# Lag blocks by way of memory and POOL's queue instead of PE, and a convolution part moved ahead, in an S5 and PEER step

## The reference

```python
def s5_scan(u, h0, ...):        # diagonal complex state space, one direction
    bu = einsum("gnp,blgp->blgn", b_bar, u)
    a_cum, h = associative_scan(_combine, (a, bu), reverse=reverse, axis=1)
    h = h + a_cum * h0
    return einsum("gpn,blgn->blgp", c_mat, h).real, ...

y = y_f + y_b + d_skip * u                   # 32 groups of 16 channels
g = gelu(y);  out = g * sigmoid(g @ w_glu + b_glu)
y_conv = cb * short_conv(cc * ch, conv_w, conv_b)      # z = h @ w_in gives u, cb, cc, ch
y = concat(rmsnorm(out), rmsnorm_heads(y_conv)) @ w_out ;  x = x + g1 * y
x = x + g2 * peer(rmsnorm_mod(x))            # top-k of keys, 16 of 16384 experts per head
```

## Time and profile before

| | |
|---|---|
| median of 3 runs | 1924.06 us (1923.41 to 1924.34) |
| the profiled execution, its own time | 1922.27 us |
| its span, first to last instruction | 1920.1 us |
| PE busy | 1194.3 us, 62% |
| DVE busy | 1382.6 us, 72% |
| ACT busy | 373.5 us, 19% |
| POOL busy | 725.1 us, 38% |
| mean DMA rate | 392 GB/s |
| first gather of the PEER stage | at 215.58 us |

### The profile page before, as it was taken

One profiled execution on the slowest core, in us unless ns is written; L12 is line 12 of the kernel. 1 busy time (PEld: TensorE's weight loads), 2 busy tenths in 40 slices (PEclk: granted clock), 3 DMA queues, 4 the chain that ended last, 5 costly groups with the idle time before them and its releaser, 6 DMA issues.

```text
span 1920.1 us, 21154 instructions
## 1 busy us (share of the span) xinstructions
PE 1194.3 (62%) x7716; PEld 475.8 (25%) x7716; DVE 1382.6 (72%) x3664; ACT 373.5 (19%) x845; POOL 725.1 (38%) x666
## 2 busy tenths in 40 slices
PE   6989898999777777775543343544343454444434
PEld 3569644444322322221110000111000011111001
DVE  8968567777766766669777776677777678766664
ACT  5142441121122121111211110121111121111110
POOL 0000233344444434445434444444444354444440
PEclk9999999999878877775755555565555565555555
DMA  9855699999999999999999999999999999999994
GB/s 372 328 209 199 257 395 414 378 416 420 390 421 399 419 422 421 420 389 422 420 422 423 421 421 421 421 421 421 422 422 421 421 421 418 422 420 421 418 420 182
DMA packets 120968, 753.16 MB, mean 392 GB/s; under 512 B 12240, under 2 KB 27856, under 8 KB 33568
## 3 DMA queue, kind: packets, MB, share of 16 engines
q0 software_dynamic: 92160, 671.13, 84.5%
q1 hardware_dynamic: 28704, 80.69, 11.0%
HBM read 749.12 MB, written 11.04 MB: 396 GB/s over the span
## 4 chain that ended last, share of the span: by engine, by line
DMA 43%; PE 28%; DVE 23%; issue 2%; POOL 1%; ACT 1%; SPq 0%; DVEq 0%; POOLq 0%; ACTq 0%
DMA r<-table,gidx 31%; DVE r L1747 9%; DMA mix_r<-table,gidx 8%; PE bank L878 7%; PE bank L846 6%; PE bank L983 3%; DMA r<-w_mod 3%; DVE mix_r L1747 2%; PE bank L996 2%; PE bank L813 1%; POOL r L1935 1%; PE bank L962 1%; PE bank L855 1%; DVE i L1680 1%; PE bank L788 1%
## 5 line engine op out<-in xcount | busy, mean ns | idle before, releaser
L1935 POOL DMA_INDIRECT r<-table,gidx x542 | 607.7, 1121 | 865.3 <-PE bank L878 723.9
L1747 DVE CUSTOM_DVE_ANT_0 r<-r 128x1024 f32<-128x1024 f32 x542 | 658.1, 1220 | 246.5 <-DMA r<-table,gidx 246.0
L878 PE MATMUL bank<-r,cond 128*32 128x512 f32 x1432 | 327.2, 911 | 370.4 <-DVE cond L1759 295.2
L878 PE MATMUL bank<-r,wgt 128*32 128x512 f32 x736 | 166.8, 921 | 194.1 <-DVE wgt L1759 145.8
L1289 ACT ACTIVATE r<-r 128x2 f32<-128x2 f32 x320 | 65.1, 204 | 1013.1 <-DVE r L1747 1012.5
L878 PEld LDWEIGHTS bank<-r,cond 128*32 128x32 f32 x1432 | 37.1, 129 | 572.0 <-DVE cond L1759 437.2
L1935 POOL DMA_INDIRECT mix_r<-table,gidx x98 | 109.4, 1116 | 136.1 <-PE bank L878 117.0
L1747 DVE CUSTOM_DVE_ANT_0 mix_r<-mix_r,r 128x1024 f32<-128x1024 f32 x98 | 119.3, 1221 | 48.4 <-DMA mix_r<-table,gidx 48.2
L878 PE MATMUL bank<-mix_r,cond 128*32 128x512 f32 x264 | 91.1, 994 | 80.7 <-DVE cond L1759 63.4
L846 PE MATMUL bank<-hT_r,r 128*128 128x512 f32 x256 | 121.5, 630 | 0.9 <-ACT hT_r L1143 0.9
L878 PEld LDWEIGHTS bank<-r,wgt 128*32 128x32 f32 x736 | 18.9, 130 | 295.3 <-DVE wgt L1759 214.3
(11 more groups left out here) (367 smaller groups left out, 1637.1 us busy)
## 6 DMA issues: line engine op xcount, KB each, us to landing
r<-w_mod SPq DMA_DIRECT2D x24, 1024.0 KB, 9.7
r<-wq_heads SPq DMA_DIRECT2D x14, 1024.0 KB, 8.8
r<-table,gidx POOLq DMA_INDIRECT x542, 18.7
wq_heads<-w_query SPq DMA_DIRECT2D x8, 1024.0 KB, 12.1
r<-w_tiles SPq DMA_DIRECT2D x12, 512.0 KB, 7.8
x_r<-w_tiles SPq DMA_DIRECT2D x10, 512.0 KB, 6.0
hT_r<-xT SPq DMA_DIRECT2D x4, 640.0 KB, 6.1
r<-w_u SPq DMA_DIRECT2D x1, 2048.0 KB, 29.5
```

Of the source, the lines that this page charges most:

```text
L878: last = mm(bank[ACC[b % 2][h]][to:to + TG, :], pair_weights(NPR * G + g)[:, e, :], rows[SLOT[G * TOPK + k]][:, D + h * 512:D + (h + 1) * ...
L1747: V.tensor_tensor_reduce(row, row, h2r[tg], 1.0, 0.0, ALU.mult, ALU.add, hid[:, par, k:k + 1]).then_inc(dot_done, 1)
L1935: G_.indirect_dma_start(rows[SLOT[j]], None, table, bass.IndirectOffsetOnAxis(gidx[:, e, k:k + 1], 0)).then_inc(row_in[SLOT[j]], 16)
```

## The change

Four things are done together.

1. PE computes the products of the lag blocks before the chunk sums instead of after them, and DVE's `lag_blocks()` stands ahead of the scan instead of between its third and fourth step.
2. M is no longer made by PE and ACT. POOL writes `Ksb` to `kfull` in device memory with one DMA (512 pieces of 960 bytes), waits for it, and reads it back with 8 DMAs, each into 16 rows of M (16 x 32 pieces of 512 bytes, 0.26 MB). PE waits for all nine ahead of the context's output.
3. The odd steps 9, 11, 13 and 15 of the chunk sums are evicted by DVE (`s_back`) instead of ACT. In each scan step two products over half the width become one over the full width, with the halves read in reverse.
4. `conv_ctx(0)` moves from behind the context's output to ahead of it, ahead of slabs 20 to 22. ACT's copy `ccx` moves with it.

```diff
@@ SP
-            sp.wait_ge(m_mm, 2)
+            sp.wait_ge(lag_dma, 16)
             sp.dma_start(wqa, w_query[:, :, 0:DQ]).then_inc(ld_first, 16)
@@ PE
             mod_slab(16)
 
-            pe.wait_ge(bpt_ev, 17)
-            for g in range(16):
-                if g >= 2:
-                    pe.wait_ge(s_ev, g - 1)
...
             pe.wait_ge(bd_ready, 1)
             pe.wait_ge(cp_ready, 1)
             pe.wait_ge(dm_ready, 1)
...
                 last.then_inc(k_mm, 1)
+
+            pe.wait_ge(bpt_ev, 17)
+            for g in range(16):
+                if g >= 10 and g % 2:
+                    pe.wait_ge(s_back, (g - 9) // 2)
+                elif g >= 2:
+                    pe.wait_ge(s_ev, min(g - 1, 4 + g // 2))
...
+                last.then_inc(s_mm, 1)
+                if g == 7:
+                    mod_slab(17)
             mod_slab(18)
             mod_slab(19)
-            pe.wait_ge(k_ev, 1)
-            pe.wait_ge(s_ev, 16)
-            for a in range(2):
-                for s in range(Q):
...
-                last.then_inc(m_mm, 1)
-                mod_slab(20 + a)
-            mod_slab(22)
...
-                pe.wait_ge(m_ev, (1, 2, 5)[r])
...
-            pe.wait_ge(m_ev, 8)
+            conv_ctx(0)
+            mod_slab(20)
+            mod_slab(21)
+            mod_slab(22)
+            pe.wait_ge(lag_dma, 16 * (Q + 1))
+            pe.wait_ge(s_ev, 12)
+            pe.wait_ge(s_back, 4)
+            pe.wait_ge(k_ev, 1)
             pe.wait_ge(hbc_ready, 1)
...
-            conv_ctx(0)
             pe.wait_ge(yc_gelu, 2)
@@ ACT
-            for g in range(16):
+            for g in (*range(8), *range(8, 16, 2)):
...
-            for n in range(8):
-                a, j = n // 4, n % 4
-                act.wait_ge(m_mm, a + 1)
-                A(M[:, 2 * j + a::8, :], bank[MBANK[a][j]][:, :].rearrange("p (q x) -> p q x", q=4), ACT.Copy).then_inc(m_ev, 1)
+            act.wait_ge(zc_mm, 4)
+            A(ccx.rearrange("p k t -> p (k t)"), bank[0][:, :], ACT.Copy).then_inc(ccx_ev, 1)
             act.wait_ge(scan_ctx, 1)
...
-            act.wait_ge(zc_mm, 4)
-            A(ccx.rearrange("p k t -> p (k t)"), bank[0][:, :], ACT.Copy).then_inc(ccx_ev, 1)
@@ DVE
-                link(tt(ta, prev, re, ALU.mult),
-                     tt(tb[:, :, 0, :], prev[:, :, 1, :], im[:, :, 0, :], ALU.mult),
-                     tt(tb[:, :, 1, :], prev[:, :, 0, :], im[:, :, 1, :], ALU.mult))
+                link(tt(ta, prev, re, ALU.mult), tt(tb, prev[:, :, ::-1, :], im, ALU.mult))
...
-            dve.wait_ge(s_ev, 16)
+            lag_blocks()
+            for g in range(9, 16, 2):
+                pr = g % 8 * 2
+                dve.wait_ge(s_mm, g + 1)
+                for r in range(2):
+                    src = bank[4 + g % 2][:, 0:4 * NCH].rearrange("p (q r c) -> p c r q", q=2, r=2)[:, :, r, :]
+                    V.tensor_copy(HH[:, NCC:0:-1, r, 1, pr:pr + 2], src[:, 0:NCC, :])
+                    last = V.tensor_copy(HH[:, NCH - 1:NCC:-1, r, 1, pr:pr + 2], src[:, NCC + 1:NCH, :])
+                last.then_inc(s_back, 1)
+            dve.wait_ge(s_back, 4)
+            dve.wait_ge(s_ev, 12)
...
-                if i == 3:
-                    lag_blocks()
...
-                     tt(seg_b[:, :, 0, :], last[:, :, 1, :], PI, ALU.mult), tt(seg_b[:, :, 1, :], last[:, :, 0, :], PI, ALU.mult))
+                     tt(seg_b, last[:, :, ::-1, :], PI.rearrange("p i (a x) -> p i a x", a=1).broadcast_to([P, SEG, 2, NQ]), ALU.mult))
@@ POOL
             pool.sem_inc(bd_ready, 1)
 
+            pool.wait_ge(k_ev, 1)
+            G_.dma_start(kfull.rearrange("(m p) x -> p m x", p=P), Ksb).then_inc(lag_dma, 16)
+            pool.wait_ge(s_mm, 8)
+            pool.wait_ge(lag_dma, 16)
+            lags = kfull.rearrange("(g i) x -> i g x", i=GC)
+            for i in range(Q):
+                G_.dma_start(M[GC * i:GC * i + GC, :, :], lags[:, :, (Q - 1 - i) * GC:(Q - 1 - i) * GC + P]).then_inc(lag_dma, 16)
+
             pool.wait_ge(mod_tr, 6)
```

More of the change, by code:

```diff
@@ L291, in build @@
         d_mm = sem("d_mm")
-        m_mm = sem("m_mm")
-        m_ev = sem("m_ev")
+        lag_dma = sem("lag_dma")
+        s_back = sem("s_back")
         s_mm = sem("s_mm")
@@ L621, in _ @@
             mod_slab(16)
-            pe.wait_ge(bpt_ev, 17)
-            for g in range(16):
-                if g >= 2:
-                    pe.wait_ge(s_ev, g - 1)
-                for j in range(2):
-                    q = 2 * g + j
-                    for r in range(2):
-                        for a in range(2):
[L631 to L635, removed]
             pe.wait_ge(bd_ready, 1)
@@ L647, in _ @@
                 last.then_inc(k_mm, 1)
+            pe.wait_ge(bpt_ev, 17)
[4 more added lines that the diff above has]
+                    pe.wait_ge(s_ev, min(g - 1, 4 + g // 2))
+                for j in range(2):
+                    q = 2 * g + j
+                    for r in range(2):
+                        for a in range(2):
+                            last = mm(bank[4 + g % 2][64 * a:64 * a + 64, (2 * j + r) * NCH:(2 * j + r + 1) * NCH],
+                                      BPT[:, q, r, 64 * a:64 * a + 64], U[:, 2 * (q % NPAIR) + a, :], start=True, stop=True)
+                last.then_inc(s_mm, 1)
+                if g == 7:
+                    mod_slab(17)
             mod_slab(18)
             mod_slab(19)
-            pe.wait_ge(k_ev, 1)
-            pe.wait_ge(s_ev, 16)
-            for a in range(2):
-                for s in range(Q):
[L656 to L663, removed]
-                last.then_inc(m_mm, 1)
-                mod_slab(20 + a)
-            mod_slab(22)
             def conv_ctx(r):
-                pe.wait_ge(m_ev, (1, 2, 5)[r])
                 for i in range(4):
```

## The result

The changed kernel takes 1939.59 us (median of 4 runs, 1935.07 to 1939.71), the kernel before on the same chip 1923.74 us (1922.78 to 1924.34). The ratio is 1.008, with a 95% interval of 1.0066 to 1.0093: 15.9 us slower. The forecast was 1929.6 us with a range of 1921.5 to 1937.0. The sign was right, the size three times too small, and the time lies outside the range. The profiled execution took 1939.65 us, its span 1937.8.

A forecast was written before the change was run, and what follows sets the result against it. The prediction took PE's path to L716 as the bound, with M late by POOL's issue: 4.1 us past break-even plus 1.4 for the clock, +5.5 on 1924.06, giving 1929.6 us, range 1921.5 to 1937.

The forecast's parts named there:

- The end follows L716 one for one: DMA-bound PEER stage: whatever the front part gains or loses at PE's L716 moves the end equally.
- The DVE path: Scans on DVE up to L716: later start +3.3 or +4.9, `lag_blocks()` out -3.1, merged products -1.9; -1.7 or 0 us.
- the issue gap: PE's 1.60 us instruction-stream gap between lag products, expected within the chunk sums in the new order; 0 or 1.6 us on top.
- When M is there: Store and eight loads on POOL's queue: 2.8 us per issue chosen, M landed at 147.6; low 130.8, high 156.2.
- the loads are slow at their destination: Rival: loads into 16 rows run at a quarter of 422 GB/s; +9 to +18 us, 1933 to 1942; chance 0.13.
- The slabs of the modulation have 5 us of cover.: PE ahead of the context's output: slab 22 is done by 138, and its coming late costs nothing below 5 us.
- The sign that I had named: New profile: PE's context output waits for a DMA of `kfull`, later than 143.5 us.
- The list of what could go wrong: Other ways to be wrong: slower scan step from reversed halves, DVE slowed by POOL, PE's slabs waiting for M's loads.
- L716 comes at Y + 24.8: PE path: from the context's output start, 24.8 us through Gelu, turn, slab 23, `conv_ctx(1)` and GLU to L716.
- Y: Start of the context's output on PE; 137.58 before the change, 147.6 forecast.
- the break-even of 143.5: Start of the context's output after which the PE path is later than before; forecast 4.1 us past it.
- the low clock, for which 1.4 were forecast: PE idle some 9 us behind slab 22, granted clock falling to 0.50; the next eight products cost 1.4 us more.

The follow-up runs named there:

- the slabs behind: Changed kernel with slabs 20 and 21 right behind the context's output, 22 and 23 behind `conv_ctx(1)`, loads 22 and 23 later; 1933.15 us, ratio 1.0044.
- 32 loads: Against the kernel with the slabs behind: M loaded by 32 DMAs into 128 rows instead of eight into 16 rows; 1930.35 us, ratio 1.0035.
- the kernel with both cures: Changed kernel with M's loads into 128 rows, and the four slabs' products and loads behind the context's output; 1924.00 us, ratio 1.000.
- the experiment that held SP's burst back: Changed kernel with one SP wait moved: gated unit weight loads and all later loads issued only after the context's output; 1934.96 us, ratio 1.006.

## Why the prediction was wrong

**The end follows L716 one for one.** Right for this kernel: +16.8 us there, +16.9 at the first gather, +15.9 in the time. In the ten others the first gather moved with L716 within 0.2 us, but for two (3.1 us more with the slabs behind, 1.0 more with 32 loads), and the medians agree with the gather's shift within 4 us.

**The DVE path, "-1.7 or 0 us".** Nearly right. The lag products took 3.70 us, the chunk sums started at 108.06 (108.2 forecast), and the issue gap did move into them, as 0.51 and 0.45 us. The scan started at 122.79, 0.4 us beyond the forecast 120.8 to 122.4, because the evictions on two engines gave nothing: the last eight chunk sums took 6.7 us (0.45 of it the issue gap) and not 5.3. The merged products gave 0.07 us a step for 0.06. The scan's end moved by some +0.3 us, and -0.6 in the kernel with both cures.

**"When M is there", 147.6.** M landed at 148.0, and this is luck: the terms were wrong and cancelled. For the issue I took 2.8 us "since piece count is what the two share"; it is 0.63, below my own lower bound of 0.94. For the landing of the last load I took 4.4 us; it was 24.2. The store took 8.4 for 4.9, which made up for its cheaper issue, so that the first load went out at 119.4 for 118.4. **This is the step that failed**: the price of the loads was looked for in POOL's issue, when it lay in the width of the destination. The rival "the loads are slow at their destination" had the mechanism, the quarter rate (105 GB/s measured) and a time of 1933 to 1942; it got a chance of 0.13. Its own sum for M alone is 142.8 us, and 141.5 was measured.

**"The slabs of the modulation have 5 us of cover."** The second failure, and it added to the first. That cover was read from a trace in which their loads landed in 5 to 10 us. Beside the narrow loads, two took 19.73 and 24.4 us. So not M but slab 22, whose load had to wait for slab 20, set the output's start: 152.55 is 4.5 us after M, and taking the slabs away moved the output by 5.8 us. The sign that I had named, an output that waits for a DMA of `kfull`, did not come. The list of what could go wrong has "PE's slabs kept waiting by M's loads", without a price in the sum.

**"L716 comes at Y + 24.8."** Y is 152.55, 9.0 us past the break-even of 143.5, and from there it took 32.6 us, not 24.8. Of the 7.8 us more, 5.0 are the two stops, a term that the sum did not have; the experiment that held SP's burst back took 3.4 of them away. The rest, 2.8 us, stands in these places: the output without its stops +1.28, the turn and slab 23 +1.77 (the turn took 1.97 for 1.04 us, slab 23 1.94 for 1.07, at a granted clock of 0.52 from 166 to 172 us), `conv_ctx(1)` +0.48, less 0.41 in the wait for Gelu and 0.30 behind. I put it down to the low clock, for which 1.4 were forecast; no run isolates it.

The sum of what was measured: 9.0 + 7.8 = 16.8 us, for 4.1 + 1.4. Of the 9.0, 4.5 are M's lateness, which the forecast had at 4.1, and 4.5 are the slabs.

## What to carry to other kernels

Before work is moved from an engine to DMAs, look at how many rows of on-chip memory each transfer writes, not only at bytes, pieces and issues: eight loads into 16 rows each ran at 105 GB/s with all DMA engines busy, and cost every other load beside them its time. Ask of each wait that seems covered whether the cover was measured with the new traffic present. When four edits come together, time the smallest alone: the merged products by themselves were the only kernel with a gain, a small one, and within the whole change it could not be seen.

## What the runs showed of the hardware

- The width of the destination sets the rate of such loads: slowest landing of eight loads of 256 KB 24.2 us at 16 rows, 15.2 at 32, 10.7 at 128, with the slab loads beside them; and loads beside the narrow ones slow down too (a packet of 8192 bytes took 677 ns for 309).
- A direct DMA from POOL's queue takes 0.63 us to issue with 512 pieces into 16 rows, 0.75 with 512 pieces into 128 rows and 0.61 to 0.95 with 128 pieces, so the count of pieces does not set it. From ACT's queue one issue lasted 8.8 us.
- PE's instruction fetches seem to go through the same DMA engines as the loads. That is my reading of stops of 2.5 us at a time beside 4 MB of loads, which shrank to 0.8 us when 3 MB of them were held back, and which end 2.4 to 2.7 us after a packet of 16 KB starts. They stood in the middle of products whose operands were all there.
- A DVE operation over reversed halves (a negative step between two rows of 128 elements) runs as fast as one without: 418 ns over 256 elements, against 425 ns for the operations without it.
